# RWKV group norms of a four-tile mixer moved behind the whole state chain, in a two-block fp32 transformer kernel

## What is computed

```python
    def step(state, inp):
        r_t, w_t, k_t, v_t, kk_t, a_t = inp
        sa = jnp.einsum('bhvk,bhk->bhv', state, -kk_t)
        state = (state * w_t[:, :, None, :] + sa[..., None] * (kk_t * a_t)[:, :, None, :]
                 + v_t[..., None] * k_t[:, :, None, :])
        return state, jnp.einsum('bhvk,bhk->bhv', state, r_t)
    ...
    mu_y = jnp.mean(y, axis=-1, keepdims=True)
    var_y = jnp.mean(jnp.square(y - mu_y), axis=-1, keepdims=True)
    y = ((y - mu_y) * lax.rsqrt(var_y + RWKV_GN_EPS)).reshape(b, s, RWKV_WIDTH) * gn_g + gn_b
    bonus = jnp.sum(rh * kh * r_k, axis=-1, keepdims=True) * vh
    y = (y + bonus.reshape(b, s, RWKV_WIDTH)) * g
```

## Time and profile before

| what | us |
|---|---|
| median of 3 runs | 3245.09 (3244.75 to 3252.64) |
| the profiled execution, its time | 3237.92 |
| the profiled execution, its span | 3236.1 |
| scan and norms, first RWKV layer | 1809.6 to 1844.7 |
| scan and norms, second RWKV layer | 2740.4 to 2775.5 |

### The profile page before, as it was taken

The page is one execution under the profiler, slowest core; times in us unless marked ns, Lnnn a source line. Parts: engine busy times, 40 slices in busy tenths (PEclk is TensorE's granted clock), DMA queues, the critical chain, the costliest instruction groups (busy, mean ns, idle before and its releaser), DMA issues.

```text
span 3236.1 us, 45287 instructions
## 1 busy us (share of the span) xinstructions
PE 2867.1 (89%) x19896; PEld 2373.6 (73%) x19896; DVE 1567.7 (48%) x2442; ACT 1033.7 (32%) x1538; POOL 266.7 (8%) x254
## 2 busy tenths in 40 slices
PE   7987999999888999999759689999898668789997
PEld 5876788878777888887548578888675558578885
DVE  3576533345574434333465554444533474654435
ACT  3324422232333222222342234223423422232323
POOL 0200000001100000000514200000003243000000
PEclk9968999999879999999869789999899779789998
DMA  4101222222003222221000123232210000223221
GB/s 163 53 1 62 78 104 91 98 74 90 14 1 116 99 97 93 94 92 52 1 1 4 54 89 104 92 104 83 79 65 14 1 2 4 91 78 104 91 98 46
DMA packets 30726, 216.59 MB, mean 67 GB/s; under 512 B 3649, under 2 KB 3777, under 8 KB 6081
## 3 DMA queue, kind: packets, MB, share of 16 engines
q1 hardware_dynamic: 30528, 213.69, 18.8%
HBM read 211.58 MB, written 2.10 MB: 66 GB/s over the span
## 4 chain that ended last, share of the span: by engine, by line
PE 80%; DVE 14%; ACT 4%; issue 1%; DMA 0%; DVEq 0%; SPq 0%; ACTq 0%
PE PS L505 76%; DVE SC L1174 3%; PE PS L508 3%; DVE SM L1185 2%; DVE R L1174 1%; DVE SM L1174 1%; DVE X L1174 1%; ACT SPL L1907 1%; DVE SPL L1174 1%; ACT LN L1907 1%; PE PS L963 1%; PE PS L1009 0%; DVE LN L1174 0%; DVE SM L1179 0%; DVE X L1179 0%
## 5 line engine op out<-in xcount | busy, mean ns | idle before, releaser
L505 PE MATMUL PS<-H,SPL 128*128 128x512 f32 (+1 forms) x4560 | 1051.3, 391 | 9.1 <-DVE SPL L1174 5.6
L505 PEld LDWEIGHTS PS<-H,SPL 128*128 128x128 f32 (+1 forms) x4560 | 851.3, 187 | 195.0 <-issue 9.7
L1174 DVE TENSOR_TENSOR SPL<-RAW,SPL 128x2048 fp32r<-128x2048 f32 (+2 forms) x194 | 434.2, 2240 | 794.1 <-ACT SPL L1907 794.1
L1907 ACT ACTIVATE SPL<-RAW 128x2048 fp32r<-128x2048 f32 (+2 forms) x194 | 362.0, 1869 | 910.1 <-PE PS L505 875.8
L505 PE MATMUL PS<-SPL,Uu 128*128 128x512 f32 x2592 | 589.8, 389 | 0.0
L505 PEld LDWEIGHTS PS<-SPL,Uu 128*128 128x128 f32 x2592 | 486.5, 188 | 101.0
L505 PE MATMUL PS<-SPL,H 128*128 128x512 f32 (+2 forms) x2112 | 463.4, 381 | 26.4 <-DVE SPL L1174 25.7
L505 PEld LDWEIGHTS PS<-SPL,H 128*128 128x128 f32 x2112 | 389.4, 193 | 99.9 <-issue 27.9
L1907 ACT ACTIVATE R<-PS 128x512 f32<-128x512 f32 (+2 forms) x180 | 104.6, 583 | 310.7 <-PE PS L505 310.6
L1174 DVE TENSOR_TENSOR X<-X,PS 128x512 f32<-128x512 f32 x112 | 76.7, 685 | 115.7 <-PE PS L505 115.7
L505 PEld LDWEIGHTS PS<-R,SC 64*64 64x64 f32 (+1 forms) x1920 | 107.9, 158 | 20.7 <-issue 13.2
(11 more groups left out here) (207 smaller groups left out, 2708.0 us busy)
## 6 DMA issues: line engine op xcount, KB each, us to landing
RAW<-in_wA SPq DMA_DIRECT2D x84, 1024.0 KB, 4.8
RAW<-in_wB SPq DMA_DIRECT2D x84, 1024.0 KB, 4.8
RAW<-in_wAo SPq DMA_DIRECT2D x8, 1024.0 KB, 4.8
RAW<-in_wBo SPq DMA_DIRECT2D x8, 1024.0 KB, 5.5
LN<-in_ln SPq DMA_DIRECT2D x4, 1024.0 KB, 5.8
P<-in_pB SPq DMA_DIRECT2D x2, 1920.0 KB, 8.7
RAW<-in_wBm SPq DMA_DIRECT2D x4, 704.0 KB, 4.1
X<-in_x SPq DMA_DIRECT2D x4, 512.0 KB, 5.1
```

The source lines that it names most:

```text
L505: return pe.matmul(out, l_, r_, start=start, stop=stop)
L1174: return v.tensor_tensor(out, a, b, o)
L1907: return a.activation(out, in_, f, scale=scale)
```

## The change

On each of the four engines `post(l, t)` waits for the flag of the last tile in place of its own. For tiles 0 to 2 that is later than before; for tile 3 it is the same. Flags, semaphores, waits and instructions are otherwise unchanged.

```diff
@@ -1037,7 +1037,7 @@
             def post(l, t):
-                while ("states", t) not in flags:
+                while ("states", 3) not in flags:
                     yield
                 b = (2, 2, 4, 6)[t]
                 pe.wait_ge(s.pr_g[t], 7 * l + 7)
```

## The result

The changed kernel is slower: the ratio of its time to the kernel before is 1.0037, with a 95% interval of 1.0024 to 1.0050 (median 3256.83 us of 22 runs against 3245.58 us of 22). That is 12 us, between 8 and 16. The prediction said 16.2 us more, 3261.3 us, with a range of 3252 to 3269.

A forecast was written before the change was run, and what follows sets the result against it. VectorE's queue was taken to end each of the two 35.1 us stretches; +5.3 - 2.0 + 0.5 + 4.3 = +8.1 us a stretch, 16.2 us for both, gave 3261.3 us, range 3252 to 3269.

The forecast's parts named there:

- a: State steps: with no norm work between them, VectorE idles during TensorE's round trips; +5.3 us a stretch (+4.4 to +6.1).
- d: Stretch end: last three gate products each wait for a gate matmul through one shared bank; +4.3 us a stretch.
- b: Norms: with four tiles side by side, VectorE's waits for ScalarE are hidden; -2.0 us a stretch.
- c: Norms' first pieces: GpSimd's instructions hold up VectorE's beside them, about even; +0.5 us a stretch (-1.5 to +2.5).
- The clock rival: State steps and late gates: TensorE's clock stays up, so only 3.9 us a stretch slower, 3252.9 us; chance 0.13.
- The GpSimd rival: Norms' first pieces: GpSimd holds VectorE throughout; +10.9 us a stretch, 3266.9 us; chance 0.12.
- the state chain sets the end: Whole stretch: state chain, not VectorE's queue, sets its end, so 4.3 us a stretch faster, 3236.5 us; chance 0.03.
- the order stays the same: Whole stretch: the wait is already there, pieces come out in the same order, nothing changes; chance 0.01.

The follow-up runs named there:

- e1: Changed kernel with a PSUM bank of its own for each tile's gate matmul; ratio 1.0015 to the kernel before, stretches 37.75 and 37.91 us.
- e2: Changed kernel with GpSimd's two instructions a tile started once the tile's preparation is through; ratio 1.0032 to the kernel before, stretches 40.19 and 39.32 us.
- e3: Changed kernel with both own gate banks and GpSimd started early; ratio 0.9992 to the kernel before, stretches 34.95 and 33.73 us.
- e5: Changed kernel with each gate matmul done twice into the same bank; ratio 1.0061 to the kernel before, stretches 42.71 and 44.23 us.
- e10: Changed kernel with seven unused matmuls on TensorE ahead of the late gates; ratio 1.0030 to the kernel before, stretches 39.25 and 42.74 us.
- e4: Kernel before, with GpSimd's two instructions a tile started once the tile's preparation is through; ratio 0.9976 to the kernel before, both stretches 32.26 us.
- e11: Kernel before with tile 2's norm beside tile 3's, GpSimd early, last gate in bank 2, four unused matmuls after it; ratio 0.9951 to the kernel before.

## Why the prediction was right, point by point

**The bound** was right: VectorE's queue ends the stretch, and its work did not change. All four terms had the right sign, and a and d were the large ones.

| term, us a stretch | forecast | first layer | second layer |
|---|---|---|---|
| a, bare chain | +5.3 (4.4 to 6.1) | +4.3 | +5.5 |
| b, ScalarE hidden | -2.0 | -2.0 | -2.0 |
| c, GpSimd | +0.5 (-1.5 to 2.5) | +0.5 | +0.5 |
| d, gate chain | +4.3 | +4.5 | +4.5 |
| sum | +8.1 | +7.3 | +8.5 |
| measured stretch | | +7.0 | +8.2 |

This is the working of the measured columns. a: from the first state add to the first tile's add, 6.93 us (1815.43 to 1822.36) in place of 0.45, less 2.15. In the second layer it is 8.18 in place of 0.50. The first layer ran at full clock all along (1.00 from 1816 to 1822) and lies at the lower end of the range; in the second the clock fell midway. The forecast's middle took the clock to be mixed, and that is what the runs show: over the twelve bare chains of the six kernels that have one (after, e1, e2, e3, e5, e10) the way is 6.93 to 8.59 us, 7.86 in the mean, which makes +5.3. b: no wait for ScalarE is left, as said. c: stalls of 0.81 + 0.80 + 0.51 + 0.63 = 2.75 us in the changed kernel against about 2.26 before (2.80 against 2.29 in the second layer); e2 gives 2.75 by removal. d: 3 x (2.92 - 1.42) = 4.5 us, by removal 4.75. The rest of 0.3 us was not traced to single instructions. What the rows show is that neighbours of different tiles start about 0.1 us before the end of the one ahead, as in e1's rows above; the changed kernel has ten such pairs in a stretch, the kernel before seven.

**The total.** By the profiles +15.3 us in the stretches and +1.1 behind the fences, 16.4 us, against 16.2 forecast. By the times the difference is 8 to 16 us, middle 12. The forecast sits at the interval's upper end; the sizes of the terms were right where they can be read, and the 4 us between lie within what the untouched code varies by. The 1.1 us behind the fence was missing in the sum (it was taken as a possible gain), and the rest of 0.3 us a stretch with it; that the profile's total comes within 0.2 us of the forecast is partly luck, since the two cancel in part. One reading was off without touching the sum: TensorE idled for 21.9 us ahead of the first late gate (19.8 in the second layer), not some 12, since its matmuls for all four tiles were through early in A.

**Rivals.** The clock rival was half right in a (first layer) and wrong in d: in both layers the granted clock was 0.50 under all late gates. The GpSimd rival fell: in each layer one subtract in four lost the hand-over. That the state chain sets the end fell by VectorE's waits in the bare chain (0.8 to 1.4 us a step, where this rival wanted none) and by e3: with gates and GpSimd out of the way, a bare chain was still no gain over e4. That the order stays the same fell by the rows of the state chain.

The rule weighed at c, from the Trainium skill's SBUF — State Buffer, Who interferes with whom, is that whichever of the two issues first has the shared port pair for its whole instruction and the other is blocked. The trace agrees on both sides: the subtract of 1.49 us waited behind a GpSimd instruction, and GpSimd's of 1.60 us behind that subtract. At d, by the Trainium skill's TensorE: Matmul & The Clock Gate, The HAM clock gate, matmul activity raises the clock, and so the last gate might have come at full clock; no late gate of the changed kernel did (2.07, 2.08 and 2.08 us), but doubled ones did (1.98 us for four records).

## What to carry to other kernels

Removing a wait from a chain gains nothing if the work that it waited behind is on the engine that sets the end. Here the state chain waited behind norm work on VectorE, and that work filled the 0.8 to 1.4 us holes of the chain's round trips; with the wait gone, VectorE stood idle in them. Before moving pieces of several tiles next to each other, look for the one buffer they share: what was hidden behind a tile's work becomes a chain of hand-overs. And when an effect is a few parts in a thousand, split the profile by stage and compare the stage; here the untouched part varied by more (24 us) than the effect (12 to 16 us).

## What was not expected of the hardware

Doing the gate matmul twice cost 1.4 and 1.7 us a stretch and not 6.2, as the granted clock rose from 0.50 to 0.97 at the end of the first pair (3.69 us of unbroken work), and four records at 2.4 GHz (1.98 us) are quicker than two at 1.2 GHz (2.08 us). Matmuls without use ahead of the fence (e11) made the 32 transposes take 3.71 us in place of 5.1 to 6.3. How close ahead of the work that is to profit they have to stand is not settled. TensorE idled for 0.6 us ahead of the first late gate in e10's first layer and for 1.3 us ahead of the transposes in e11's, and the clock stayed up; it idled for 2.0 us in e10's second layer, and the clock fell just as the gate began. In the kernel before it fell 1.8 us behind the second step's last matmul (1.00 until 1813.4, 0.50 from 1813.5). An idle time isn't the whole of it, since the clock also fell under the transposes of e10's first layer, 0.9 us behind the last gate; what decides it in each case is not shown here.
